# Two decoder layers on one core: float32 scores in three rounded products, shares turned by transposes, memory-attention rounds reordered, squares added by GpSimd, first strips of the feed-forward cast early

## The reference

```
def forgetting_attention(q, k, v, c):            # 12 heads x 64, 8 blocks of 128 queries
    s = einsum(q, k) * scale + c_q - c_k         # causal, c: running sum of log forget gates
    p = softmax(s);  out = p @ v                 # then * sigmoid(gate)
def memory_attention(q_cols, mem, ...):          # 4 heads x 64 over 256 memory tokens
    s = q k^T * scale;  p = softmax(s);  out = p @ v
def merge_and_ffn(x, l, main, mem_cols):
    x = x + concat([main, mem_out]) @ w_out[l]
    return x + (silu(h @ w_gate) * (h @ w_up)) @ w_down,   h = rms_norm(x, ffn_norm[l])
# between the layers: k, v, log f = rms_norm(x, kv_norm) @ w_kv;  u = rms_norm(x, mix_norm[1]) @ b_w_in
```

## Time and profile before

| | |
|---|---|
| three runs | 2947.65, 2935.38, 2959.13 us; median 2947.65 |
| the profiled execution | 2945.26 us, of which the span is 2943.4 |
| PE, DVE, ACT, POOL busy | 94%, 63%, 41%, 46% of the span |
| mean granted clock of PE | 0.971 |

### The profile page before, as it was taken

One profiled execution on the slowest core, in us unless ns is written; L12 is line 12 of the kernel. 1 busy time (PEld: TensorE's weight loads), 2 busy tenths in 40 slices (PEclk: granted clock), 3 DMA queues, 4 the chain that ended last, 5 costly groups with the idle time before them and its releaser, 6 DMA issues. The chain is left out here.

```text
span 2943.4 us, 56612 instructions
## 1 busy us (share of the span) xinstructions
PE 2778.7 (94%) x23069; PEld 2247.1 (76%) x23069; DVE 1841.9 (63%) x2375; ACT 1198.8 (41%) x2174; POOL 1364.6 (46%) x1126
## 2 busy tenths in 40 slices
PE   7999989989889999999998999999989999999998
PEld 5888677777667788887786777766667788887787
DVE  6333566666453766656896688866643766656895
ACT  3111343333233433334444666656633433334442
POOL 6344134444242655556655354464322655556653
PEclk9999899999899999999999899999999999999999
DMA  5333100010042243335653132253122243335651
GB/s 196 107 108 106 59 25 25 25 46 4 3 136 79 79 129 112 103 108 181 192 138 97 36 95 92 87 172 130 66 87 79 79 129 113 102 107 179 194 139 68
DMA packets 290601, 295.36 MB, mean 100 GB/s; under 512 B 11623, under 2 KB 223709, under 8 KB 289193
## 3 DMA queue, kind: packets, MB, share of 16 engines
q1 hardware_dynamic: 288440, 286.89, 30.9%
q10 hardware_dynamic: 1424, 4.83, 0.4%
q0 software_dynamic: 480, 0.03, 0.0%
HBM read 200.30 MB, written 88.65 MB: 98 GB/s over the span
## 5 line engine op out<-in xcount | busy, mean ns | idle before, releaser
L312 POOL TENSOR_TENSOR w_lo_b<-w_raw_b,w_hi_b 128x512 fp32r<-128x512 f32 (+3 forms) x540 | 750.6, 1393 | 672.1 <-ACT w_hi_b L346 668.8
L396 PE MATMUL ps<-b_hi,w_hi_b 128*128 128x512 f32 x1540 | 610.3, 396 | 9.4 <-issue 9.4
L396 PE MATMUL ps<-b_lo,w_hi_b 128*128 128x512 f32 x1540 | 602.3, 391 | 0.0
L396 PE MATMUL ps<-b_hi,w_lo_b 128*128 128x512 f32 x1540 | 602.0, 391 | 0.0
L346 ACT ACTIVATE w_hi_b<-w_raw_b 128x512 fp32r<-128x512 f32 (+3 forms) x498 | 295.3, 597 | 451.8 <-PE ps L3397 196.0
L396 PEld LDWEIGHTS ps<-b_hi,w_hi_b 128*128 128x128 f32 x1540 | 291.3, 189 | 74.7 <-issue 14.9
L396 PEld LDWEIGHTS ps<-b_lo,w_hi_b 128*128 128x128 f32 x1540 | 291.4, 189 | 64.1 <-issue 3.9
L396 PEld LDWEIGHTS ps<-b_hi,w_lo_b 128*128 128x128 f32 x1540 | 291.0, 189 | 60.8
L3397 PE MATMUL ps<-b_hi,w_hi_b 128*128 128x512 f32 x616 | 245.6, 399 | 23.8 <-DVE x_res L3214 23.3
L3397 PE MATMUL ps<-b_lo,w_hi_b 128*128 128x512 f32 x616 | 242.4, 394 | 0.0
L3397 PE MATMUL ps<-b_hi,w_lo_b 128*128 128x512 f32 x616 | 242.3, 393 | 0.0
(11 more groups left out here) (431 smaller groups left out, 5749.6 us busy)
## 6 DMA issues: line engine op xcount, KB each, us to landing
w_raw_b<-in_w_gate_up SPq DMA_DIRECT2D x88, 512.0 KB, 4.4
act_dram<-x_res SPq DMA_DIRECT2D x44, 512.0 KB, 6.1
sum_dram<-x_res SPq DMA_DIRECT2D x40, 512.0 KB, 2.9
w_raw_b<-in_w_down SPq DMA_DIRECT2D x28, 512.0 KB, 5.8
stage<-sum_dram SPq DMA_DIRECT2D x54, 256.0 KB, 3.9
stage<-act_dram SPq DMA_DIRECT2D x50, 256.0 KB, 4.4
w_raw_a<-in_a_w_in SPq DMA_DIRECT2D x23, 512.0 KB, 4.8
u_dram<-evac_a SPq DMA_DIRECT2D x16, 512.0 KB, 3.1
```

The source lines that it names most:

```text
L312: nc.gpsimd.tensor_tensor(self.wlo[:, r, 0:n, :], source, self.whi[:, r, 0:n, :].bitcast(F32), ALU.subtract).then_inc(self.w_lo, 1)
L396: mm = self.nc.tensor.matmul(self.ps[:, bank, :], w[:, r, k, :], h[:, block, k, :], start=(start and k == 0 and a == 0 and h is self.bh), ...
```

## The change

Lines from L389 on stand lower in the changed kernel. The right-hand sides b_hi and b_lo become three tensors (first_b, kept_b, freed_b), and `part(lo, b)` finds a block, `strip_parts(lo, k)` the two halves of a strip; first_b is there from the out phase on. Cut to its core:

```diff
 # out: strips 0 to 3 are cast there
-nc.scalar.activation(X[:, k, :], X[:, k, :], ACT.Copy, scale=ffn_norm)
+scaled_strip = nc.scalar.activation(X[:, k, :], X[:, k, :], ACT.Copy, scale=ffn_norm)
+if k < HK:
+    scaled_strip.then_inc(scaled, 1); act.wait_ge(scaled, k + 1)
+    nc.scalar.activation(self.strip_parts(0, k), two(X[:, k, :]), ACT.Copy).then_inc(self.h_hi, 1)
 # out, DVE, in round i
+if 2 <= i < HK + 2:
+    dve.wait_ge(self.h_hi, KT - PAIRS + i - 1)
+    tt(self.strip_parts(1, i - 2), two(X[:, i - 2, :]), self.strip_parts(0, i - 2), SUBTRACT)
 # ffn, ACT
-for k in range(KT):
+for k in range(HK, KT):            # casts of strips; DVE's loop the same
-cast_sum(3)                        # ahead of the loop over f
 for f in range(1, FT):
     copy(gate(f)[:, 0, :], ps[:, b, :])
     if f == 1:
+        cast_sum(3)
         silu(0)
 # ffn down, SP
-store(FT - 1)
-residual(slice(6, 8), H2, x_late)
-sp.wait_ge(act_stored[1], 16 * (FT // 2))
-residual(slice(2, 4), H2, x_late)
 # ffn down, ACT, loop over blocks b of visit v, ahead of its cast
+if v == 1 and b == 0:
+    act.wait_ge(act_full, FT)
+    act.dma_start(two(self.act_dram[FT - 1]), up(FT - 1)).then_inc(act_stored[...], 16)
+    act.dma_start(X[:, 6:8, H2], self.x_dram[:, 6:8, H2]).then_inc(x_last_half, 16)
+if v == 1 and b == 5:
+    act.wait_ge(act_stored[1], 16 * (FT // 2))
+    act.dma_start(X[:, 2:4, H2], self.x_dram[:, 2:4, H2]).then_inc(x_last_half, 16)
 # ffn down, DVE
+scale_up_by_rms(FT - 1)
 add_product(1, 0)
+scale_up_by_gate(FT - 1)
 add_product(1, 1)
-scale_up(FT - 1)
+self.early_sums(dve, d0 + 2, (0,))
 add_product(1, 2)
-self.early_sums(dve, d0 + 2)
+self.early_sums(dve, d0 + 2, (1,))
-dve.wait_ge(x_late, 4 * 16)        # before visit 2
+dve.wait_ge(x_late, 2 * 16)
+if v == 2: dve.wait_ge(x_last_half, 2 * 16)      # before add_product(v, 2)
 # proj, POOL (acc, square: 128x1024; kept_flat: two 128x512)
+add_whole(0, 1)                    # acc += square
+add_halves(0, 2)                   # acc += kept_flat, two instructions
 for j in range(split_from, split_to):
     self.split_block(pool, j)
+    if j == first(1) + 1:
+        add_whole(1, 4); add_halves(2, 5); add_whole(3, 7)
 # proj, PE
-        if k == 0:
-            column_sums(0, early_sums_done)
+def sum_tokens():
+    pe.wait_ge(self.added, 7)
+    for t in range(TT):
+        mm = mmul(ps[:, 6, t:t + 1], acc[:, t * P:(t + 1) * P], ones, start=True, stop=True)
+late = lambda p: p > 2 and len(heads_of(p - 2)) == 2        # p = 9 and 12
-    if before:
+    if before and not late(p):
         head_sum(before[0])        # after block 0; ACT's root and DVE's division follow it
     ...product j + 1, product j + 2
+    if late(p):
+        head_sum(before[0])
 # proj, pair 1: ACT copies rms before its gains instead of before block 3's cast; ACT's square_head
 # comes before the two forget-gate operations; DVE's late_sums(2) after the second addition;
 # DVE's bias and memset of the forget gate after scale(1, 0)
 # fox, PE
-for h in range(2):
-    mm = mmul(part_bank(n, a, h), q[b][hs[h], ...], k[b][hs[h], lo:hi], start=True, stop=True)
+if p == 0: (as before)
+else:
+    for i, (x, y) in enumerate(((high, high), (high, low), (low, high))):
+        for h in range(2):
+            mm = mmul(part_bank(n, a, h), x[hs[h], 0, ...], y[hs[h], 1, lo:hi], start=(i == 0), stop=(i == 2))
-for u in range(8):
-    mm = mmul(ps[hs[u % 2], 7, ...], share[:, g % 2, u:u + 1].broadcast_to([P, HD]), ident)
+for m in range(4):
+    mm = nc.tensor.transpose(ps[:, 7, m * P:(m + 1) * P], wide_share[:, g % 2, 2 * m:2 * m + 2, :], ident)
 # fox, ACT, at blocks 3 and 5 of a pair, for the next pair's q and k
+    act.wait_ge(qk_in, 32 * p)
+    nc.scalar.activation(high[p % 2][:, m, :], (q, k)[m][p % 2], ACT.Copy).then_inc(split_hi, 1)
 # fox, POOL: widen(g) copies share to 64 columns each (128x512); low = q - high, k - high (128x1024)
 # mem, POOL
     nc.gpsimd.tensor_copy(self.hh[:, c, :], self.X[:, c, :])
+    if c not in by_vector:         # by_vector: 0, 2, 4 in mem0, none in mem1
+        nc.gpsimd.tensor_tensor(self.hl[:, c, :], self.X[:, c, :], self.hh[:, c, :], ALU.subtract)
 # mem, ACT: the copy of the spread shares moves from the end to the start of round i
 # mem, DVE: the reciprocal moves from after the copies to the start of round i, ahead of the least
```

More of the change, by code:

```diff
@@ L2628, in phase_mem_attention @@
             acts_copy = lambda n, h: h == 1 and n % 2 == 0
+            by_vector = range(0, PAIRS, 2) if layer == 0 else range(0)
             @block.sync
@@ L2695, in _ @@
                 for i in range(N + 2):
+                    if i >= 3 and i % 2 == 1:
+                        g = i // 2 - 1
+                        act.wait_ge(spread, g + 1)
+                        if g >= 2:
+                            act.wait_ge(stored, g - 1)
+                        nc.scalar.activation(scale[:, g % 2, :], shares, ACT.Copy).then_inc(scaled, 1)
                     if i < N:
@@ L2720, in _ @@
                 for i in range(N + 2):
+                    if 2 <= i <= N and i % 2 == 0:
+                        g = i // 2 - 1
+                        dve.wait_ge(exped, 2 * i)
+                        if g >= 2:
+                            dve.wait_ge(spread, g - 1)
+                        nc.vector.reciprocal(share[:, g % 2, :], total[:, g % 2, :]).then_inc(shared, 1)
                     if i < N:
```

251 lines of the change are left out of this document (151 added, 100 removed).

## The result

| | before | after |
|---|---|---|
| median (four runs each) | 2946.01 us | 2917.0 us (2911.64 to 2919.95) |
| ratio | 1 | 0.991, 95% interval 0.9887 to 0.9934 |
| profiled execution | 2945.26 us, clock 0.971 | 2919.95 us, clock 0.973 |

The changed kernel is faster by 29 us, about 1%. The forecast was 2863, with a range of 2840 to 2905: it was 54 us too low, and the measured median lies outside the range.

What follows compares the result with a forecast made beforehand. PE, busy 94% of the span, was taken as the bound, with its waits and the slow clock behind them. Gains of 10.6 + 7 + 16.8 + 15.4 + 4.3 + 7.5 + 12 + 8.5 = 82.1 us off 2945.3 gave 2863, range 2840 to 2905.

Steps and rivals of the forecast that it cites:

- First strips early: Start of ffn0 and ffn1: strips cast in the out phase let PE start with ACT, without slow clock; gain 10.6 us.
- cast_sum(3): First pair product of each ffn: this cast moved behind ACT's first copy ends PE's wait at the third block; gain 7 us.
- Down: Feed-forward down part, visits 1 and 2: last tile and half strips moved so nobody waits for x from DRAM; gain 16.8 us.
- Rival 2: Down's waits only move, to ACT's casts or late halves, and half of the gain returns: 2879 us; chance 0.12.
- Squares by GpSimd: Start of proj: GpSimd adds squares, leaving PE eight one-column sums; gain 15.4 us, beside 4.3 for pair 2's head sum.
- Head sums: Proj: shorter waits in pair 2, gain 4.3 us; sums two blocks later in pairs 9 and 12, gain 7.5 us.
- Memory rounds: Memory attention: PE's waits for reciprocals and last products go, with some slow clock; gain 12 us.
- Fox: Fox: fp32r scores with heads side by side gain 6 us, transposed shares 6, pair starts cost 3.5; net 8.5 us.
- rival 3: Fox: the two fp32r heads run one after the other; 2892 us, chance 0.07.
- rival 4: Fox: an fp32r product on 64 partitions costs several passes, so the kernel is slower, up to 3075 us; chance 0.03.
- rival 1: GpSimd is late: its additions run dearer beside DVE, costing proj 6 us, fox 9, mem0 3; 2881 us, chance 0.18.
- rival 5: Whole kernel: PE leaves each gap for another engine's next instruction, little but the removed sums (about 25) remains; 2920 us, chance 0.05.

Runs made afterwards that it cites:

- experiment 1: Changed kernel with the head sums of pairs 9 and 12 of proj back behind block 0; the pairs took 26.05 and 26.09 us, proj 5.95 us shorter.
- experiment 3: Changed kernel with ACT's cast_sum(3) ahead of the first copy again, both ffn phases; from pair 1 to pair 2 took 23.39 and 23.40 us.
- experiment 5: Changed kernel with GpSimd's seven additions at proj's start cut to 8 columns; third block began 20.68 us after the start, proj 8.8 us shorter.
- experiment 6: Changed kernel with GpSimd's five subtractions of column 2 in down cut to 8 columns; ffn0 4.1 us shorter, ffn1 5.1.
- experiment 10: Changed kernel with DVE's weight sums of the third pair ahead of sum_rest(3) and scale_up(0); from pair 1 to pair 2 took 20.51 and 20.53 us.
- experiment 9: Changed kernel with the five subtractions of column 2 in down made by DVE instead of GpSimd; both ffn phases 4.5 us shorter.
- experiment 4: Changed kernel with down's store, fetches and DVE order of visits 1 and 2 as in the kernel before; ffn0 1.43 us shorter, ffn1 0.04.
- experiment 2: Changed kernel with DVE's division in pairs 9 and 12 of proj split in halves around an addition; pairs took 24.76 and 24.83 us, proj 5.05 shorter.

## Why the prediction was wrong, step by step

**What bounds the kernel.** Right as a reading: nearly all of the change lies at gaps of PE. It failed in how a gap was priced, at what PE waited plus the slow stretch behind it. Experiments 1, 3, 5, 6 and 10 show that a gap gave only what the next late instruction left of it; in four of the seven terms that was a third at best (6.6 of 19.7), and three times a loss.

**First strips early: right, 8.8 of 10.6.** PE starts with ACT, 2.4 us earlier. The second part, 2.95 for the slow clock, came in ffn0 (2.8) but only in part in ffn1 (1.1), where a slow stretch fell again behind the start (27.2 us to pair 1 in place of 25.5). Both values turn up in the other runs, in either layer; in experiment 1 both layers had 25.5, and the term was 10.5. So the forecast's size was right and the 8.8 partly chance.

**cast_sum(3): the failed step is "the cast is needed only by the pair's last block, 10 us on".** That holds for PE. The cast's first user is DVE, whose queue runs on from its subtraction through the scaling to the weight sums; ACT waits for these ahead of a copy that PE needs. The term of 7 measured -2.7. Experiment 3 shows the sign, 10 the cause.

**Down: the failed step is "nothing is late by more than 1 us".** The landings were right, x was there. What was late next was GpSimd, which I had not laid beside DVE in these visits: the earlier trace rows show DVE idle 3.88 us for x, and just then GpSimd worked off its backlog: in that trace it has no pause from 1395.1 to 1413.2. Rival 2, "the waits in down only move", came true by another road than ACT's casts or the late halves, and it took back more than the whole term (-4.2 of 16.8) instead of half. Experiments 6 and 9 show GpSimd's load to be the cause, 4 shows that with it in place the DRAM wait had cost next to nothing.

**Squares by GpSimd: the failed step is "whose chain ... I make end near 1632".** That is 20 us after the start; it ended 31.3 after. I took DVE's durations from the rows before and let each addition stop one operation at most, in the rival alone, priced at 6 us for all seven. Measured, they stretched DVE's chain by 10.7: without them (experiment 5) the third block began 20.7 us after the start, close to the 20 of the forecast. PE's sums waited 4.3 for the additions besides, and the eight sums took 3.58 at the slow clock, not 1.8. The row that warned was there: 2.45 us for a narrow sum, as long as the addition beside it. The Trainium skill (SBUF — State Buffer, "SBUF: two separate sides") says the loser of the shared port waits for the other's whole instruction; this trace agrees: the subtraction begun at 1604.32 took 3.43 us instead of 1.23 and ended 1.1 after the addition that had begun before it. Experiment 5 confirms it. It belonged in the forecast, not in a rival at 0.18.

**Head sums: the failed step is "with nothing waiting but the next head's sum a block on".** DVE's division is 6.5 us long and in order; behind it stood the addition that the pair's last block waits for, and that block waited 4.62 (experiments 1 and 2). The other half of the error is the 3.35 itself, counted as gone: 2.17 of it came back ahead of the third block, with the same late square as its source, and experiment 2 gained nothing against the kernel before. The term of 7.5 measured -6.7. Pair 2 gained nothing either, 26.8 us against 26.3: its head sum waits 1.5 instead of 2.63, but gaps of 0.7 and 1.8 are new, the second ahead of its last block, whose addition again stands behind a division (1666.05 to 1672.6).

**Memory rounds: right, 15.6 for 12.** The waits gave 11.4 of it; of the slow stretches of 3.4 us that were counted as gone, the one inside mem0 is, the one in mem1 stayed. **Fox: right in sum, 9.4 for 8.5.** The heads run side by side in fp32r (two starts 0.003 apart, the next pair 0.23 on), so rivals 3 and 4 are out. But two errors cancel: the scores gave 4.2 instead of 6 and the shares about 4.6 instead of 6, and the pair starts cost 0.3 at most instead of 0.7 each.

**The chances.** Rivals 1 and 2 were given as alternatives, 18 and 16 us. Of rival 1 the proj part came (6 in its price), its 12 for fox and memory did not; rival 2 came, by its own road. Squares, down and the cast together lack 44 us against the forecast, more than the 34 of both rivals; the division, 14 more, was in neither. The number that comes closest is rival 5, 2920, held at 0.05: PE leaves each gap for another engine's next instruction. Its mechanism is what the four failed terms show. That its number fits is partly luck: it let only the removed sums count, about 25, while in the measured 26.8 memory, fox and the first strips are 33.8 and the other terms together -7.0. Five moves that each trust one other engine's slack should not have had 0.55 on all going well.

## What to carry to other kernels

A wait of the bound engine is worth no more than the slack of what comes second: before pricing it, lay the queues of all engines beside each other from that point on, and look for one that uses the wait to catch up. When an instruction is moved, follow its first consumer and everything behind that one in its queue, long divisions above all. Work given to GpSimd cost DVE time here where both of DVE's operands lay in SBUF and not where one was in PSUM, so ask what DVE does beside it before calling it free.
